# The shift half of a layer's first modulation as fp32 products on TensorE

## What is computed

```
cond = silu(c)                                  # c: 2048 numbers
mod  = cond @ mod_w + mod_b                     # mod_w: 2048 x 12288
sh_m, sc_m, gt_m, sh_f, sc_f, gt_f = split(mod, 6)
h = rms_norm(x, g0) * (1.0 + sc_m) + sh_m       # x: 256 x 2048
qkv = h @ w_qkv                                 # 2048 x 3072, then attention
```

## Time and profile before

| | |
|---|---|
| median of 3 runs | 1232.06 us (1229.7 to 1233.01) |
| profiled execution | 1226.82 us, its span 1225.0 us |
| busy, share of the span | PE 86%, VectorE 64%, ScalarE 39%, GpSimd 7% |
| `mraw` loads | 192 of 512.0 KB, 6.2 us to landing (median) |
| mod pieces on VectorE (L580) | two forms, 96 of each, 128.7 and 124.3 us busy |

### The profile page before, as it was taken

The page is one execution under the profiler, slowest core; times in us unless marked ns, Lnnn a source line. Parts: engine busy times, 40 slices in busy tenths (PEclk is TensorE's granted clock), DMA queues, the critical chain, the costliest instruction groups (busy, mean ns, idle before and its releaser), DMA issues.

```text
span 1225.0 us, 13423 instructions
## 1 busy us (share of the span) xinstructions
PE 1053.1 (86%) x4712; PEld 862.1 (70%) x4712; DVE 782.4 (64%) x843; ACT 476.7 (39%) x568; POOL 83.5 (7%) x57
## 2 busy tenths in 40 slices
PE   0155568797778996999999999999999999999995
PEld 0144457576656765888888888888888888888884
DVE  5777879999987868476676644444444454454544
ACT  3311232653653444433343433343334434344343
POOL 0000013313311001000000000000000000000002
PEclk9677778798878998999999999999999999999998
DMA  8998877887779962687787755555655455555541
GB/s 310 362 322 308 297 273 249 282 307 274 267 251 341 342 241 68 205 293 265 268 303 278 268 178 194 185 199 176 205 174 201 149 198 202 178 202 194 185 169 69
DMA packets 104194, 288.94 MB, mean 236 GB/s; under 512 B 6752, under 2 KB 6752, under 8 KB 97888
## 3 DMA queue, kind: packets, MB, share of 16 engines
q1 hardware_dynamic: 103152, 286.29, 67.0%
q10 hardware_dynamic: 1008, 2.23, 0.5%
HBM read 286.39 MB, written 2.10 MB: 235 GB/s over the span
## 4 chain that ended last, share of the span: by engine, by line
PE 65%; DVE 16%; DMA 9%; issue 5%; ACT 4%; POOL 1%; ACTq 0%; SPq 0%; DVEq 0%
PE ps L1095 21%; PE ps L1097 21%; PE ps L1096 21%; DMA mraw<-in_mod_w 8%; DVE mraw L580 5%; DVE wlo L569 5%; ACT whi L312 2%; ACT s L368 1%; PE ps L1117 1%; DMA sinkp<-in_sinks 1%; DVE hf L842 1%; DVE qr L648 1%; PE ps L1214 0%; DVE qr L654 0%; PE ps L1234 0%
## 5 line engine op out<-in xcount | busy, mean ns | idle before, releaser
L569 DVE TENSOR_TENSOR wlo<-raw,whi 128x2048 fp32r<-128x2048 f32 x172 | 395.2, 2299 | 312.1 <-ACT whi L312 312.0
L1095 PE MATMUL ps<-whi,hThi 128*128 128x512 f32 x1248 | 497.6, 399 | 94.0 <-DVE wlo L569 88.7
L312 ACT ACTIVATE whi<-raw 128x2048 fp32r<-128x2048 f32 x172 | 328.7, 1913 | 466.5 <-PE ps L1097 455.7
L1096 PE MATMUL ps<-wlo,hThi 128*128 128x512 f32 x1248 | 492.9, 395 | 0.0
L1097 PE MATMUL ps<-whi,hTlo 128*128 128x512 f32 x1248 | 492.5, 395 | 0.0
L1095 PEld LDWEIGHTS ps<-whi,hThi 128*128 128x128 f32 x1248 | 238.9, 191 | 150.7 <-issue 91.1
L1097 PEld LDWEIGHTS ps<-whi,hTlo 128*128 128x128 f32 x1248 | 238.7, 191 | 50.9
L1096 PEld LDWEIGHTS ps<-wlo,hThi 128*128 128x128 f32 x1248 | 239.2, 192 | 49.2
L580 DVE CUSTOM_DVE_ANT_0 mraw<-mraw,cb,modT 128x1024 f32<-128x1024 f32 x96 | 128.7, 1358 | 36.0 <-DMA mraw<-in_mod_w 35.8
L580 DVE CUSTOM_DVE_ANT_0 mraw<-mraw,cb,mbias 128x1024 f32<-128x1024 f32 x96 | 124.3, 1311 | 41.2 <-DMA mraw<-in_mod_w 30.2
L1095 PE MATMUL ps<-whi,oThi 128*128 128x512 f32 x128 | 53.6, 419 | 6.3 <-DVE wlo L569 3.6
(11 more groups left out here) (131 smaller groups left out, 543.6 us busy)
## 6 DMA issues: line engine op xcount, KB each, us to landing
mraw<-in_mod_w SPq DMA_DIRECT2D x192, 512.0 KB, 6.2
raw<-in_w_in SPq DMA_DIRECT2D x88, 1024.0 KB, 5.1
raw<-in_w_out SPq DMA_DIRECT2D x44, 1024.0 KB, 4.8
raw<-in_w_qkv SPq DMA_DIRECT2D x24, 1024.0 KB, 8.7
raw<-in_w_o SPq DMA_DIRECT2D x16, 1024.0 KB, 8.5
x<-in_x ACTq DMA_DIRECT2D x2, 1024.0 KB, 11.9
x<-in_x SPq DMA_DIRECT2D x2, 1024.0 KB, 8.2
out<-x SPq DMA_DIRECT2D x8, 256.0 KB, 2.6
```

The source lines that it names most:

```text
L312: A(whi[:, s % 2], raw[:, s], ACT.Copy).then_inc(hi_done, 1)
L569: V.tensor_tensor(wlo[:, s % 2], raw[:, s], whi[:, s % 2].bitcast(F32), ALU.subtract).then_inc(lo_done, 1)
L1095: mm(dst, hi, whi[:, s % 2, n], start=start, stop=False)
L1096: mm(dst, hi, wlo[:, s % 2, n], start=False, stop=False)
```

## The change

The shift columns (n even, n < 8) no longer go to VectorE.

- The host gives the shift part of `mod_w` in its natural layout, `mod_sh`: for each quarter c eight pieces of the same 128 x 1024, now 128 input rows by 512 outputs, two such blocks to a piece. `ccz` holds silu(c) by columns: for each of the 16 blocks of 128 inputs a 128 x 32 tile whose first column is the values and whose rest is zero.
- PE (`shift`) multiplies each block as fp32, 512 columns, with output in the 32 PSUM partitions from 32 (k mod 4) of bank 6, so that four column groups each collect four blocks. ScalarE (`shift_out`) copies the bank to `gacc`. PE (`shift_columns`) sums over the partitions with four products of one column against `ones` into bank 7, and VectorE adds the bias into `modT` at the start of `modulate`.
- The transposes of `x` use six banks in place of eight.
- SP waits on `g_step`, which PE raises for each shift piece, for a buffer that a shift piece held. The order of its loads and their sizes stay.
- VectorE runs quarter by quarter: eight scale pieces, `modulate(c)`, `hTlo`, three `wlo`. Nothing of quarter c + 1 stands ahead of `modulate(c)`.
- PE runs quarter 0's shift pieces ahead of the transposes. Pieces 0 and 1 of quarter c + 1 stand ahead of quarter c's third block, pieces 2 to 7 behind it.

```diff
@@ load_m
-                if not first:
-                    sp.wait_ge(acc_step, MPN * n + j - 3)
+                early = isinstance(n, int) and n < 8
+                if early and j < 4 and n % 2:
+                    sp.wait_ge(g_step, MPN * (n // 2) + j + 5)
+                elif early and j >= 4 and not n % 2:
+                    sp.wait_ge(g_step, MPN * (n // 2) + j - 3)
+                elif early and j < 4 and n:
+                    sp.wait_ge(acc_step, dve_pieces(n - 1) + j + 5)
+                elif not first:
+                    sp.wait_ge(acc_step, dve_pieces(n) + j - 3)
...
@@ scalar
+            def shift_out(c):
+
+                act.wait_ge(g_step, MPN * (c + 1))
+                if c:
+                    act.wait_ge(reduced, c)
+                A(gacc[:, :], ps[:, 6], ACT.Copy).then_inc(g_evac, 1)
+
+            shift_out(0)
             for c in range(4):
                 act.wait_ge(hf_done, c + 1)
                 A(hThi[:, 4 * c:4 * c + 4], nT[:, 4 * c:4 * c + 4], ACT.Copy).then_inc(hhi_done, 1)
                 for g in range(3 * c, 3 * c + 3):
                     hi(g // 4, g % 4)
+                if c < 3:
+                    shift_out(c + 1)
...
@@ vector
-            first_mod(0, range(4, 8))
+            first_mod(1, range(4, 8))
...
             def modulate(c):
                 ks = slice(4 * c, 4 * c + 4)
-                dve.wait_ge(acc_step, MPN * (2 * c + 2))
+                dve.wait_ge(reduced, c + 1)
+                V.tensor_tensor(modT[:, ks], ps[:, 7, 0:4], mbias[:, ks], ALU.add).then_inc(mod_added, 1)
+                dve.wait_ge(mod_added, c + 1)
+                dve.wait_ge(acc_step, MPN * (c + 1))
...
@@ tensor
+            def shift(c, js):
+
+                for j in js:
+                    pe.wait_ge(m_loaded[j % 4], 16 * (4 * c + j // 4 + 1))
+                    if c and j == 0:
+                        pe.wait_ge(g_evac, c)
+                    for t in range(2):
+                        k = 2 * j + t
+                        row = 32 * (k % 4)
+                        last = mm(ps[row:row + 32, 6], ccz[:, k], mraw[:, j % 4, t * N:(t + 1) * N],
+                                  start=k < 4, stop=k >= 12)
+                    last.then_inc(g_step, 1)
+
+            def shift_columns(c):
+
+                pe.wait_ge(g_evac, c + 1)
+                if c:
+                    pe.wait_ge(mod_added, c)
+                for f in range(4):
+                    last = mm(ps[:, 7, f:f + 1], gacc[:, f * P:(f + 1) * P], ones[:, 0:1], start=True, stop=True)
+                last.then_inc(reduced, 1)
+
+            pe.wait_ge(silu_c, 1)
+            shift(0, range(8))
...
             for c in range(4):
+                shift_columns(c)
                 pe.wait_ge(h_ready, c + 1)
                 for e in range(3):
                     g = 3 * c + e
+                    if e == 2 and c < 3:
+                        shift(c + 1, range(0, 2))
                     project(g // 4, c, hThi, hTlo, 2 * e, half_done, slot=g % 4)
+                if c < 3:
+                    shift(c + 1, range(2, 8))
```

More of the change, by code:

```diff
@@ L60, in after, with build @@
     return q + (s + n) // 4, (s + n) % 4
-def build(nc, x, crow, pos, invf, mod_w, modbT, gT, w_qkv, w_o, sinks, w_in, w_out, out):
+def build(nc, x, crow, cT, mod_sh, pos, invf, mod_w, modbT, gT, w_qkv, w_o, sinks, w_in, w_out, out):
     with ExitStack() as ctx:
@@ L114, in build @@
         freq = at("freq", 74, [P, HALF])
+        ccol = at("ccol", 0, [P, KT])
+        ccz = at("ccz", 1, [P, KT, 32])
+        gacc = at("gacc", 4, [P, N])
         oThi = at("oThi", 0, [P, KT, T], F32R)
@@ L153, in build @@
         acc_step = sem("acc_step")
+        cz_zero, g_step, g_evac, reduced, mod_added = (
+            sem(n) for n in ("cz_zero", "g_step", "g_evac", "reduced", "mod_added"))
         c_in, k_in, x_in, x1_in = sem("c_in"), sem("k_in"), sem("x_in"), sem("x1_in")
@@ L186, in piece_of, with dve_pieces @@
             return 2 * (j // 4) + j % 2, j // 2 % 2
+        def dve_pieces(n):
+            return MPN * (n // 2 if isinstance(n, int) and n < 8 else n - 4)
         block = ctx.enter_context(nc.Block())
@@ L200, in load_m @@
             def load_m(n, j, col=None, first=False):
-                if not first:
-                    sp.wait_ge(acc_step, MPN * n + j - 3)
+                early = isinstance(n, int) and n < 8
[7 more added lines that the diff above has]
+                    sp.wait_ge(acc_step, dve_pieces(n) + j - 3)
                 c = n if col is None else col
                 f, half = piece_of(j)
-                src = mod_w[bass.ds(4 * c + f, 1), :, half * MHALF:(half + 1) * MHALF]
-                sp.dma_start(mraw[:, j % 4], src.rearrange("a p k -> p (a k)")).then_inc(m_loaded[j % 4], 16)
+                if early and not n % 2:
+                    src = mod_sh[c, j]
+                else:
+                    src = mod_w[bass.ds(4 * (c - SC_M) + f, 1), :, half * MHALF:(half + 1) * MHALF]
+                    src = src.rearrange("a p k -> p (a k)")
+                sp.dma_start(mraw[:, j % 4], src).then_inc(m_loaded[j % 4], 16)
             def block_src(w, r, col):
                 return w.rearrange("(r t p) n -> r p t n", p=P, t=WP)[r][:, :, bass.ds(col, N)]
+            sp.dma_start(ccol[:, :], cT).then_inc(c_in, 16)
             sp.dma_start(cb[:, :], crow).then_inc(c_in, 16)
@@ L318, in _ @@
                 act.dma_start(x0[:, b], x[b * P:(b + 1) * P, :]).then_inc(x_in, 16)
-            act.wait_ge(c_in, 16)
+            act.wait_ge(c_in, 32)
+            act.wait_ge(cz_zero, 1)
+            A(ccz[:, :, 0], ccol[:, :], ACT.Silu).then_inc(silu_c, 1)
             A(cb[:, :], cb[:, :], ACT.Silu).then_inc(silu_c, 1)
@@ L575, in mod @@
                 c = n if col is None else col
+                done = dve_pieces(n)
                 dst = modT[:, bass.ds(4 * c + f, 1)]
@@ L578, in mod @@
                 if half:
-                    dve.wait_ge(acc_step, MPN * n + j - 1)
+                    dve.wait_ge(acc_step, done + j - 1)
                 V.tensor_tensor_reduce(mraw[:, j % 4], mraw[:, j % 4], cb[:, half * MHALF:(half + 1) * MHALF],
@@ L590, in link @@
                 dve.wait_ge(setup, count[0])
+            V.memset(ccz[:, :, :], 0.0).then_inc(cz_zero, 1)
             V.memset(ones[:, :], 1.0)
@@ L602, in first_mod @@
                     mod(n, j, (SH_M, SC_M)[n % 2] + n // 2 if n < 8 else n)
-            dve.wait_ge(silu_c, 1)
+            dve.wait_ge(silu_c, 2)
             dve.wait_ge(k_in, 80)
-            first_mod(0, range(0, 4))
+            first_mod(1, range(0, 4))
             link(V.tensor_copy(posf[:, :], posi[:, :]))
@@ L655, in rope_parts @@
                 yield
+            dve.wait_ge(sines, 2)
+            V.tensor_copy(ropeC[:, :, HALF:], ropeC[:, :, 0:HALF])
+            V.tensor_scalar(ropeS[:, :, 0:HALF], ropeS[:, :, HALF:], -1.0, None,
+                            ALU.mult).then_inc(tables, 1)
+            dve.wait_ge(nT_done, 8)
             for c in range(4):
                 if c:
[L659 to L682, removed]
+                    first_mod(2 * c + 1, range(0, 8))
+                modulate(c)
+                if c == 3:
+                    first_mod(8, range(0, 2))
+                h_lo(c)
+                for g in range(3 * c, 3 * c + (2 if c == 3 else 3)):
+                    lo(g // 4, g % 4)
             dve.wait_ge(h_ready, 4)
             V.memset(s1[:, :, :, 0:CHUNK], 0.0).then_inc(zeros, 1)
-            first_mod(8, range(3, 5))
+            first_mod(8, range(2, 5))
             lo(2, 3)
@@ L868, in _ @@
             lo(9, 3)
-            dve.wait_ge(acc_step, MPN * 20)
+            dve.wait_ge(acc_step, dve_pieces(20))
             V.scalar_tensor_tensor(acol[:, :], modT[:, 4 * KT:5 * KT], 1.0, gcol[:, 2], ALU.add,
@@ L926, in _ @@
                 f1(i, False, True, False)
-            dve.wait_ge(acc_step, MPN * 24)
+            dve.wait_ge(acc_step, dve_pieces(24))
             dve.wait_ge(diag_done, 2)
@@ L1123, in _ @@
                 for r in range(4):
+                    if 4 * b + r >= 6:
+                        pe.wait_ge(nT_done, 4 * b + r - 5)
                     for t in range(4):
-                        last = turn(ps[:, 4 * b + r, t * P:(t + 1) * P], x0[:, b, (4 * r + t) * P:(4 * r + t + 1) * P])
+                        last = turn(ps[:, X_BANKS[4 * b + r], t * P:(t + 1) * P], x0[:, b, (4 * r + t) * P:(4 * r + t + 1) * P])
                     last.then_inc(xt, 1)
@@ L1355 @@
 POOL_ADDS = (3, 2)
+X_BANKS = (0, 1, 2, 3, 4, 5, 0, 1)
 F_MOD = [(0, 1), (2,), (3,), (4, 5), (6,), (7,), (), ()]
```

9 lines of the change are left out of this document (6 added, 3 removed).

## The result

The changed kernel takes 1272.47 us (1271.51 to 1273.08), the kernel before 1232.09 on the same chip: a ratio of 1.033, 95% interval [1.0312, 1.0348], some 40 us slower. 1276 was forecast, with 1257 to 1296 as the range.

The account below looks back on a forecast made before the run. Bound: transfers held up by when each of four `mraw` ring buffers comes free. Three cycles +42.1 and the start +1.4 make 43.5 us; on the profiled 1226.8 that gives 1270, with 5.2 for the median 1276 (range 1257 to 1296).

Parts of the forecast that it names:

- The saving: 32 of 192 mod pieces leave VectorE, 39 us of its time; none gained as such, since no byte less is loaded.
- The price of a piece on PE: Each shift piece, two fp32 products in two of four column groups, was to cost PE 0.87 us.
- lower bound: A shift piece costs PE 0.43 us if the next piece's two column groups run beside it too.
- (d): Cycle step: shift pieces 0 and 1 on PE, between the second and third product blocks, 1.7 us.
- (g): Cycle's last step: from shift piece 7's end, scale piece 3, a weight and scale pieces 4 to 7, 15 us.
- The rule of the Trainium skill: Each of a shift piece's four records adds a weight load: +2.7 us a cycle, 1284; within Rival 1's 0.18.
- The walk: Step-by-step sum of one new cycle, from one scale piece 7's end to the next: 49.6 us, three cycles +42.1.
- The ends: Outside the cycles: first `modulate` +1.4 us as `stat` stands behind scale piece 7; `modulate(3)` to the split 0, later code 0.
- The 5.2 us: Added to 1270 because the median before stood 5.2 us above the profiled execution, giving 1276.
- Rival 1: Column groups run one after another, or at low clock: 1.73 us a piece, +13 us, 1289; 0.18 in either form.
- Rival 3: DMA engines saturate in the cycles as VectorE's relief lets the ring run: 29.1 us a cycle, 1214; chance 0.04.

Follow-up runs that it names:

- x1_pe_first: The changed kernel with all eight shift pieces of quarter c+1 ahead of quarter c's first product block on PE: 1239.54 us.
- x5_own: The changed kernel, all orders kept, with eight further buffers for the shift pieces, so that `mraw`'s four serve VectorE's pieces alone: 1215.48 us.
- y1_before_own: The kernel before, all sums on VectorE and all orders kept, with only the eight further buffers of x5_own: 1225.53 us.
- x2_one_group: The changed kernel with all shift products in one column group, output always in PSUM partitions 0 to 31: 1293.68 us.
- x4_stat_early: The changed kernel with VectorE's `stat` moved ahead of scale pieces 0 to 3: 1262.05 us.
- x6_first_split: x1_pe_first with VectorE taking scale pieces 0 to 3 of quarter c+1 ahead of its third `wlo` of quarter c, 4 to 7 behind: 1216.48 us.
- y2_own_mid: x5_own plus x6_first_split's VectorE order and x4_stat_early's edit; shift pieces 0 to 3 between PE's first and second block, 4 to 7 before the third: 1199.33 us.
- the last two variants: x5_own with x6_first_split's VectorE order and x4_stat_early's edit, 1203.57 us; and the same with PE's shift pieces moved between blocks (y2_own_mid), 1199.33 us.
- x3_twice: The changed kernel with every shift product issued twice in its group and the sum halved by ScalarE: 1279.19 us.

## Why the prediction was right, point by point

**What bounds the kernel.** It named the moment when a ring buffer comes free rather than VectorE's load. x1_pe_first (release moved, 33 us back) and x5_own (release made harmless, 57 us back) show it. In both VectorE has the changed kernel's work and order.

**The saving is not gained as such.** VectorE has 6 to 9 us less to do in each cycle, and the kernel is slower. y1_before_own adds what the prediction did not say: with separate buffers on both sides, the 39 us that leave VectorE are worth some 10 us.

**The price of a piece on PE.** The value taken, 0.87 us, was too high and its lower bound right: two pieces take 1.07 us, four 1.92. I had counted two groups side by side from the earlier trace rows and took the next piece's groups to follow; x2_one_group shows all four together. In (d) this mattered little, 0.7 us a cycle, and (g), short by 1.0, made it good. The rule of the Trainium skill that I weighed ("TensorE: Matmul & The Clock Gate", packing small matmuls: weight loads overlap products only across row groups) is not what these runs show; the same section also names a load into the array's background weight buffer as one that is pulled ahead, which these rows do not rule out. In x2_one_group all records have the same rows and the same columns, each needs its load of 0.11 us, and they still follow each other at the pace of 2 x 512 columns at 2.4 GHz, 0.43 us, but for the first. The same page gives a speedup of 2.38 for three column groups, 0.79 for each; the 3.4 for four here are 0.85 for each.

**The walk.** 49.6 us a cycle against 49.9, 48.8 and 49.1; three cycles were to cost 42.1 us over before, and from the first row of the four `nT` operations (L636, now L675) to the fourth they cost 41.1 (147.8 against 106.7). The first half is right nearly part by part: SP issues nothing from shortly before `modulate` until the shift pieces behind the second block, and the DMA engines stand idle meanwhile. The second half is right as a sum and wrong in its path: it went through the landing of shift piece 6 and pieces 6 and 7 on PE, and the trace's chain goes from piece 5 to the landing of scale piece 0. That the two ways are within 1 us of each other is luck. The rate was to be near 235 GB/s: the second and third cycle have 230 and 238, the first 175, since what SP had queued had landed before it began (1 GB/s from 52.3 to 60).

**The ends.** `modulate(0)` was to start 1.4 us later and starts 0.9 later (52.7 against 51.8, the first row of the four `nT` operations), and x4_stat_early confirms that `stat`'s place holds it. From `modulate(3)` to the split 0 was forecast; it is 18.0 us for 17.3, +0.7. Behind the stage 0 was forecast too, and the profiled executions differ by +2.0 there (1051.3 for 1049.3 us). I put no cause to it: in the experiments the length from the rotation of the keys to the end scatters from 1045.9 (x5_own) to 1052.1 (x1_pe_first), where the code is the same. Together 0.9 + 41.1 + 0.7 + 2.0 = 44.7 us, the difference of the two spans, 1269.7 - 1225.0. The medians differ by 40.4. The profiled execution of before, 1226.82 us, is faster than any other run of that kernel on record (1227.53 is the next). The walk is made of the changed kernel's own lengths, so what it forecasts is the profiled time: 1270 against 1271.5. The 5.2 us added for the median supposed that the changed kernel's median would stand as far above the walk; it stands 1 us above the profiled execution, and this alone puts the 1276 some 4 us too high. Where the 5.2 us of before lie is not shown.

**The rivals.** Rival 1's price, +13, was too low for what it described: x2_one_group costs 21. The walk had counted five pieces of a cycle, 0.87 us more each. Measured, each of the eight costs some 1.25 us more (1.75 to 1.8 for 0.5): the two between the blocks take 3.6 us, and pieces 2 to 7 run without a gap for 10.5, so that pieces 3 to 5 no longer hide under piece 6's landing. Quarter 0's eight add 2.8 at the start (`modulate(0)` at 55.5 for 52.7). Rival 3 was right to be called excluded for this order, and x5_own, x6_first_split and the runs after them show that the loss turns into a gain when PE no longer holds the buffers. Its cycle of 29.1 us at the saturated rate was not reached: in y2_own_mid the rate is there, 402 GB/s, and PE's chain holds the cycle at 31.

## What to carry to other kernels

When work moves to another engine, follow the buffers it reads, not the busy time it frees: its place in the new engine's queue decides when they are released, and the loads behind them wait with it. Ask what the queue that issues the loads waits for, and what stands ahead of that in the other engine's list. If a ring is shared by two consumers, either take its pieces in the order in which they land, on both, or give each its own; here the one or the other turned a loss of 3.3% into a gain of 1.2 to 1.3%.

Do not read the bound from a full row. In the last two variants the DMA engines are busy all the time, and yet it is TensorE's chain that ends last. And when a walk's sum comes out, compare its path with the chain of waits too.

## What the runs showed of the hardware

Products in four column groups of 32 run side by side as fp32: 8 records of 512 columns in 1.07 us, against 3.62 in one group.

TensorE's clock falls behind such products as well. In the changed kernel (columns as in the earlier trace rows, the clock after POOL; the last row is of the timeline):

```profile
78.60:80.50 1.90, 1.90 (x17) 0.42 (x16) 0.00 (x0) 0.00 (x0) 0.00 (x0) 1.00 0.00 0
80.50:83.00 2.50, 0.05 (x4) 0.00 (x0) 0.00 (x0) 0.00 (x0) 0.00 (x0) 0.99 0.88 324
83.00:86.20 3.20, 3.19 (x8) 0.38 (x8) 0.00 (x0) 0.00 (x0) 0.00 (x0) 0.50 0.88 303
84.30 0.19 PEld L1155 LDWEIGHTS ps<-mraw,ccz 128*32 128x32 f32 x4 [1.11 <-DMA mraw<-in_mod_sh]
```

After 2.5 us without work it was at 1.2 GHz. The last two shift pieces of the cycle then took 3.2 us, where two at 2.4 GHz took 1.07. Part of that is a wait: the last row shows that piece 7's weight loads came at 84.3, when its transfer had landed. From there its four records took 1.9 us at a granted clock of 0.50, as long as the eight of the same piece in x3_twice at 1.00, where PE had stood idle for 1.5 us and the clock had not fallen. I had taken the higher clock for them and 0.9 us each; since the chain does not go through these two pieces, this cost the kernel little or nothing that the trace shows.

Given the buffers, the DMA engines keep 402 GB/s over a whole cycle of 31 us (y2_own_mid), the rate that in the kernel before showed only ahead of the cycles (401 from 35 to 50 us); in the cycles it moved 300 to 314.
